# Two more tiles held back at the end of a feed-forward layer, and weight tiles split inside the transposition stage

## What is computed

```python
def conv_ffn(h, w_in, conv_w, conv_b, w_out):
    u = h @ w_in
    a, b = u[..., :D_FF], u[..., D_FF:]
    a = lax.conv_general_dilated(a, ...) + conv_b
    return (jax.nn.gelu(a) * b) @ w_out

for i in range(DEPTH_2):
    mod = (c_act @ mod_w[i] + mod_b[i]).reshape(B, 6, D)[:, :, None, :]
    hin = x * (1.0 + mod[:, 1]) + mod[:, 0]
    y = ...                                   # mixer i
    x = layer_norm(DEEPNORM_ALPHA * x + mod[:, 2] * y, ln_g[i, 0], ln_b[i, 0])
    hin = x * (1.0 + mod[:, 4]) + mod[:, 3]
    y = conv_ffn(hin, ffn_w_in[i], ffn_conv_w[i], ffn_conv_b[i], ffn_w_out[i])
    x = layer_norm(DEEPNORM_ALPHA * x + mod[:, 5] * y, ln_g[i, 1], ln_b[i, 1])
```

## Time and profile before

| | us |
|---|---|
| runs | 922.94, 928.46, 928.64 |
| median | 928.46 |
| the profiled execution | 925.36 |
| its span in the trace | 923.6 |

### The profile page before, as it was taken

The page is one execution under the profiler, slowest core; times in us unless marked ns, Lnnn a source line. Parts: engine busy times, 40 slices in busy tenths (PEclk is TensorE's granted clock), DMA queues, the critical chain, the costliest instruction groups (busy, mean ns, idle before and its releaser), DMA issues.

```text
span 923.6 us, 14524 instructions
## 1 busy us (share of the span) xinstructions
PE 884.4 (96%) x5776; PEld 763.0 (83%) x5776; DVE 689.9 (75%) x1077; ACT 449.7 (49%) x712; POOL 92.7 (10%) x71
## 2 busy tenths in 40 slices
PE   8999999998998899989999999989999899999996
PEld 8988877666776687769999999858997799999995
DVE  4697789788787777779968768877877796646667
ACT  5563554444354554445554454344554565445550
POOL 2000001000000211013201201021000140100101
PEclk9999999999899999999999999999999999999999
DMA  7855567546769470197978779728813967664601
GB/s 286 325 165 175 190 220 253 176 131 212 252 222 386 161 261 13 58 361 273 354 260 265 281 242 360 249 92 317 298 47 131 365 235 256 204 206 150 207 10 46
DMA packets 56892, 200.74 MB, mean 217 GB/s; under 512 B 6588, under 2 KB 7924, under 8 KB 56824
## 3 DMA queue, kind: packets, MB, share of 16 engines
q1 hardware_dynamic: 55816, 196.63, 60.5%
q0 software_dynamic: 1008, 3.18, 1.1%
HBM read 198.71 MB, written 1.08 MB: 216 GB/s over the span
## 4 chain that ended last, share of the span: by engine, by line
PE 81%; DVE 11%; ACT 3%; issue 3%; DMA 1%; POOL 0%; SPq 0%; DVEq 0%; ACTq 0%
PE ps L1092 24%; PE ps L1093 24%; PE ps L1094 23%; PE ps L1265 4%; DVE wsp L1323 2%; PE ps L1286 2%; DVE wk L1359 1%; DVE R L1384 1%; PE ps L1272 1%; PE ps L1105 1%; PE ps L1226 1%; DVE arena L1384 1%; DMA ring<-in_w_iq 1%; DVE X L1756 1%; DVE XT L1366 0%
## 5 line engine op out<-in xcount | busy, mean ns | idle before, releaser
L1092 PE MATMUL ps<-XT,wsp 128*128 128x256 f32 x776 | 219.8, 283 | 3.3 <-DVE XT L1366 1.5
L1093 PE MATMUL ps<-XT,wsp 128*128 128x256 f32 x776 | 216.7, 279 | 0.0
L1094 PE MATMUL ps<-XT,wsp 128*128 128x256 f32 x776 | 216.4, 279 | 0.0
L1323 DVE TENSOR_TENSOR wsp<-ring,wsp 128x1024 fp32r<-128x1024 f32 x137 | 169.4, 1247 | 10.9 <-ACT wsp L1854 10.9
L1854 ACT CAST wsp<-ring 128x1024 fp32r<-128x1024 f32 (+1 forms) x136 | 141.8, 1046 | 73.5 <-PE ps L1094 63.7
L1092 PEld LDWEIGHTS ps<-XT,wsp 128*128 128x128 f32 x776 | 145.5, 188 | 7.8 <-issue 3.3
L1093 PEld LDWEIGHTS ps<-XT,wsp 128*128 128x128 f32 x776 | 145.4, 187 | 0.8
L1094 PEld LDWEIGHTS ps<-XT,wsp 128*128 128x128 f32 x776 | 145.3, 187 | 0.0
L1323 DVE TENSOR_TENSOR wsp<-arena,wsp 128x1024 fp32r<-128x1024 f32 x70 | 95.7, 1376 | 11.2 <-ACT wsp L1854 11.2
L1092 PE MATMUL ps<-wsp,ra 128*128 128x512 f32 x240 | 96.7, 403 | 6.2 <-DVE ra L1351 4.4
L1094 PE MATMUL ps<-wsp,ra 128*128 128x512 f32 x240 | 96.0, 400 | 0.0
(11 more groups left out here) (264 smaller groups left out, 1554.5 us busy)
## 6 DMA issues: line engine op xcount, KB each, us to landing
arena<-in_mod_w SPq DMA_DIRECT2D x49, 512.0 KB, 6.1
ring<-in_mod_w SPq DMA_DIRECT2D x43, 512.0 KB, 4.6
ring<-in_ffn_a SPq DMA_DIRECT2D x34, 512.0 KB, 4.7
ring<-in_ffn_b SPq DMA_DIRECT2D x24, 512.0 KB, 5.2
ring<-in_ffn_o SPq DMA_DIRECT2D x22, 512.0 KB, 4.6
arena<-in_ffn_o SPq DMA_DIRECT2D x22, 512.0 KB, 4.7
arena<-in_ffn_b SPq DMA_DIRECT2D x20, 512.0 KB, 4.7
ring<-in_w_moz SPq DMA_DIRECT2D x13, 512.0 KB, 4.6
```

The costliest lines, as they stand in the source:

```text
L1092: pe.matmul(o, l[0], r[0], start=start, stop=False)
L1093: pe.matmul(o, l[0], r[1], start=False, stop=False)
L1094: return pe.matmul(o, l[1], r[0], start=False, stop=stop)
L1323: ve.tensor_tensor(w[:, 1024:1024 + n], raw[slot[0]][:, 0:n], w[:, 0:n].bitcast(f32), SUB).then_inc(*done("V", "lo", u, also=[("raw", *slo ...
```

## The change

Layer 0 now holds back four tiles of `w_out` (18 to 21). They are taken for rows 0 first: tiles 18 and 19 in both column halves, then 20 and 21 by column halves as before. For rows 1 tiles 18 and 19 come next, each in both column halves, and their two buffers are given back there; then 20 and 21 by column halves. Layer 1 is as it was. A new method `ahead` prepares one further tile (load, high half) and puts out one low half, if a buffer is free. `modulated` calls it twice in each of the four transitions: behind the second group of modulation tiles, ahead of the transposes of t = 1, and behind the `xt_lo` that follows the `xt_m` of k = 4. At m10 the modulation tiles are divided 1, 4, 3 instead of 3, 3, 2.

```diff
-LAST = [10, 8]
+LAST = [9, 8]
...
+        def ahead(self):
+
+            if part.free and len(self.ready) < len(units):
+                self.prepare()
+                self.low()
+
...
-    def transposed(tag, nk, kind, ks=None, apart=False, filled=()):
+    def transposed(tag, nk, kind, ks=None, apart=False, filled=(), mid=None):
...
                 pending.append((k, s))
                 if len(pending) > 1:
                     low_part()
+                if mid and k == 4:
+                    mid()
         while pending:
             low_part()
...
         v.tiles(tiles[0])
-        transposed(f"m{i}{which}", 8, "m", apart=True, filled=(lambda: v.tiles(tiles[1]), lambda: v.tiles(tiles[2])))
+        transposed(f"m{i}{which}", 8, "m", apart=True, filled=(lambda: (v.tiles(tiles[1]), W.ahead()),
+                                                               lambda: v.tiles(tiles[2])), mid=W.ahead)
         v.end()
...
             for cb in range(2):
                 for j in js[-2:]:
                     piece(0, cb, j)
+            free = js[:-2] if i == 0 else []
+            for j in free:
+                for cb in range(2):
+                    piece(1, cb, j)
+                W.done(got[j][1])
             for cb in range(2):
-                for j in js:
+                for j in js[len(free):]:
                     piece(1, cb, j)
-            for j in js:
+            for j in js[len(free):]:
                 W.done(got[j][1])
...
-    modulated(1, 0, late[0], (3, 3, 2))
+    modulated(1, 0, late[0], (1, 4, 3))
```

## The result

| | us |
|---|---|
| changed kernel, median of its runs (lowest to highest) | 928.02 (926.90 to 932.03) |
| kernel before, median of the runs beside it (lowest to highest) | 925.14 (922.83 to 928.64) |
| ratio, with its 95% interval | 1.0036 (1.0024 to 1.0047) |
| span of the profiled execution, after / before | 926.8 / 923.6 |

By the ratio the change costs 3.3 us of the time before; the two medians lie 2.9 us apart. The forecast, 928.5, is near 928.02 for two errors that cancel: it set the kernel before at 928.46, the median of three runs, where more runs give 925.14, and it added 0.05 where 3.3 belongs.

What follows compares the result with a forecast made beforehand. TensorE's work was taken as the time, so only its idle at the four transitions could change. Terms -2.5 + 0.65 + 1.25 + 0.65 = 0.05 us, added to the median 928.46, gave 928.5 us; range 921.5 to 933.

Steps and rivals of the forecast that it cites:

- Step 1, the end of the layer: Ahead of m10: TensorE waits about 0.95 us for GpSimd, yet the t = 1 transposes start 0.8 us earlier.
- Step 2, the held turns: At m10: two held `mod_v` come out together, `mod_one` waits 1.7 to 2.6 us; cost +1.25 us.
- Step 3, m00: At m00: pairs brought forward remove a 1.91 us wait for a low half and the slow clock behind it; -2.5 us.
- Step 3, m01 and m11: At m01 and m11: pairs brought forward only cost, 0.19 us and 0.45 us of wait, about +0.65 us each.
- the weighing of the clock: At m10 and ahead of 328: waits from about 1.9 us may halve the clock, making the sum 3.3 us.
- rival C: Slower by the clock: it falls at 617 and ahead of 328; +3.3 us, 931.8; chance 0.22.
- A: Gains and costs over the four transitions cancel, -2 to +2 us; likeliest, chance 0.50.

Runs made afterwards that it cites:

- turn_early, turn_early: The changed kernel with `mod_v` (1,3,6) put out earlier, at the start of `last`; ratio 1.0011 to the kernel before.
- pair_m10: The kernel before with both `ahead` calls at transition m10 alone; ratio 1.0009 to the kernel before.
- first_m01_m11: The kernel before with only the first `ahead` call, at m01 and m11 alone; ratio 1.0031 to the kernel before.
- pairs_m01_m11: The kernel before with both `ahead` calls at m01 and m11 alone; ratio 1.0040 to the kernel before.
- ahead_m00: The kernel before with both `ahead` calls at m00 alone; ratio 0.9987 to the kernel before.
- both_early: early_no_m01_m11 with `mod_v` (1,3,7) also put out early, in VectorE's pause at m10; ratio 0.9980 to the kernel before.
- cover: both_early with tile 18 taken for rows 1 before tiles 20 and 21 are taken for rows 0; ratio 0.9967 to the kernel before.
- ahead_only: The kernel before with the `ahead` calls at all four transitions and nothing else; ratio 1.0025 to the kernel before.
- early_no_m01_m11: turn_early with the `ahead` calls kept at m00 and m10 alone; ratio 0.9981 to the kernel before.
- after_no_m01_m11: The changed kernel with the `ahead` calls kept at m00 and m10 alone; ratio 1.0010 to the kernel before.
- second_m01_m11: The kernel before with only the second `ahead` call, at m01 and m11 alone; ratio 1.0012 to the kernel before.

## Why the prediction was right or wrong

**Step 1, the end of the layer: right.** TensorE waits 0.79 us for GpSimd (0.95 forecast), VectorE waits for TensorE before `res_m` (1,0), and the transposes start after an idle of 2.33 us (2.35 forecast). Timeline of VectorE in after, to be laid beside the earlier trace rows:

```profile
598.69 0.69 DVE L1761 TENSOR_TENSOR wk<-ps,R 128x512 f32<-128x512 f32 x1 [0.89 <-PE ps L1108]
...
613.09 0.69 DVE L1380 TENSOR_TENSOR XT<-wk,XT 128x512 fp32r<-128x512 f32 x1 [1.48 <-ACT XT L1907]
613.69 1.22 DVE L1337 TENSOR_TENSOR wsp<-ring,wsp 128x1024 fp32r<-128x1024 f32 x1
614.83 1.28 DVE L1398 SCALAR_TENSOR_TENSOR arena<-arena,cactr 128x1024 f32<-128x1024 f32 x1
616.22 1.28 DVE L1398 SCALAR_TENSOR_TENSOR arena<-ring,cactr,arena 128x1024 f32<-128x1024 f32 x1
```

**Step 2, the held turns: right, in order and size.** Both `mod_v` stand behind one low half and `mod_one` starts 1.39 us later (1.25 forecast) after a wait of 2.65 us (1.7 to 2.6). turn_early confirms the cause by itself.

**Step 3, m00: right, 0.4 us too small.** 2.9 us against 2.5, the same in four kernels. The wait of 1.91 us and the fall behind it are gone (3.7 us by the product of 316.06, 3.6 forecast), and a wait of 2.0 us stands before the product of 330.45, as foreseen.

**Step 3, m01 and m11: the waits right, the whole wrong.** Without a fall the price is 0.18 + 0.48 us at m01 (0.19 + 0.45 forecast), each term from the call it was put down to, and 0.18 + 0.47 at m11. In the changed kernel's profile m11 shows 0.3 because 0.39 us come back behind it: from 733 to about 750 us its products follow each other faster. Seven of the fourteen profiles show that, pair_m10 and first_m01_m11 among them and pairs_m01_m11 not, so it isn't put down to an edit. What failed is the weighing of the clock: I asked for waits of 1.9 us or more and looked at m10 and 328 alone. The wait at m01 that grew from 0.99 to 1.17 us wasn't looked at, and the kernels with it lose 2 us more than the waits are long, most of it clock.

**The sum and the clock.** The terms without new falls come to -2.9 + 0.66 + 1.39 + 0.65, -0.2 us; 0.05 was forecast. But rival C, at 0.22, is what the profile shows and not A, at 0.50: falls at 328 and 618, the two places it named, and +3.3 us by the ratio, its very figure. The reason that I gave against it, that TensorE is busy for 5.6 us ahead of the wait at 617, did not hold the clock there. That the figure fits is partly luck: the profile has a third new fall, at 410, and two of before are gone, of which that at 606 had cost 0.3 us (the kernel before with it has a stretch of 255.69 us, ahead_m00, the same kernel at m10, without it 255.41), because TensorE was waiting there anyway. Nor does a wait decide by its length: the 2.0 us ahead of 328 brought a fall in the profiles of after, both_early and cover and none in those of turn_early, ahead_only, ahead_m00, early_no_m01_m11 and after_no_m01_m11. The three with it are also the three with a fall at 283 to 284, where all kernels are the same, and those whose fall near 231 starts latest (at 232.02 us or later; at 231.85 or earlier in the other eleven). So whether the wait at 328 brings a fall goes with the state in which an execution arrives there, and no profile shows m00 without the calls in that state. The Trainium skill (TensorE: Matmul & The Clock Gate, What's actually happening) calls the throttled state the default, released by activity. The falls behind the waits at 328 and 618 agree with that.

**The base.** Three runs of before, 5.7 us apart, were taken as they stood. The profiled execution, 925.36 us, was the better base: 925.14 is the median of more runs. With it and the forecast of +0.05 the prediction would have been 925.4, 2.6 us too low.

## What to carry to other kernels

A pause of an engine is filled at no cost only by an instruction that is shorter than the pause: here 1.22 us in 0.86, at two places, cost 0.4 us of wait and 2.9 us in all, of which about half is clock, while the same move at m00, where it took away a wait of 1.91 us, paid. When tasks run beside a loop by a rate, lengthening the stretch in which they are held makes them come out together afterwards: find the reader of the last one. And where the clock falls in some executions and not in others, one profile of each kernel doesn't settle a few microseconds: compare the mean clock over the timed runs too.

## What the runs showed of the hardware

**GpSimd's subtraction is slower beside VectorE's.** It was not in the prediction. In first_m01_m11 the low half of k = 4 runs alone, timeline of GpSimd:

```profile
411.09 1.30 POOL L2170 TENSOR_TENSOR XT<-wk,XT 128x512 fp32r<-128x512 f32 x1 [6.01 <-ACT XT L1905]
```

and in second_m01_m11 VectorE's low half of a weight tile started 0.22 us ahead of it, timelines of VectorE and GpSimd:

```profile
410.32 1.22 DVE L1335 TENSOR_TENSOR ra<-ring,ra 128x1024 fp32r<-128x1024 f32 x1
...
410.54 2.16 POOL L2170 TENSOR_TENSOR XT<-wk,XT 128x512 fp32r<-128x512 f32 x1 [5.83 <-ACT XT L1905]
```

The same instruction takes 1.30 and 2.16 us, 0.86 us more; when it starts, VectorE's 1.22 us have 1.00 left. In the changed kernel it takes 2.15 to 2.16 us at all four transitions (1.29 to 1.30 in before), 3.4 of the 7.0 us by which GpSimd is busy longer. The products that read it come 0.17 us later for it (in second_m01_m11 and pairs_m01_m11), but the split of k = 6 comes later still and sets the 0.48 us, so it adds nothing here. The Trainium skill (SBUF — State Buffer, SBUF: two separate sides) says that the two engines share a port pair which one of them holds for a whole instruction while the other is blocked, and names a VectorE instruction with two inputs in SBUF against a GpSimd one that reads SBUF, as here. These rows agree, but the added time is 0.14 us less than VectorE's rest.

**Falls of the clock** were 3.4 us long each at m00, m01 and m10 (once two behind each other, from 605 in second_m01_m11, whose stretch is 1 us longer for it), and each cost 1.5 to 1.6 us where products set the time (1.05 net at m01, 0.3 at m10's transposes, where a wait vanishes in it or TensorE waits anyway). The same wait brings one in one profiled execution and not in another, and in the kernels where a wait is 1.17 us in place of 0.99 they are more frequent (mean clock 0.9886 and 0.9907). Why that small step matters is open: no run here tells the wait's length from the place of its neighbours (0.41, 0.73 and 0.51 us at m01).
